# RWKV rounds of a hybrid decoder layer: activation functions grouped by table, the inversion's second half moved four slots, and two small reorderings

## The reference, cut to what matters

```
w_log = -softplus(-(w0 + tanh(xw) @ w2)) - 0.5 ; decay = exp(-exp(w_log))
a = sigmoid(a0 + xa @ a2) ; g = sigmoid(xg) @ g2
kk = k*k_k ; kk = kk * rsqrt(sum(kk*kk) + 1e-12) ; k = k*(1 + (a-1)*k_a)
# per token:  S = S diag(w) + (S a) b^T + v k^T ;  y = S r
y = (y - mean(y)) * rsqrt(var(y) + eps) * ln_w + ln_b + sum(r*k*r_k)*v
out = (y * g) @ w_out
```

## Time and profile before

| | us |
|---|---|
| median of 3 runs (lowest, highest) | 4605.08 (4598.61, 4607.50) |
| profiled execution, its own time | 4614.81 |
| its span | 4613.1 |
| PE busy | 4125.8 (89%) |
| DVE busy | 2521.4 (55%) |
| ACT busy | 1557.5 (34%) |
| mean granted TensorE clock | 0.95 |

### The profile page before, as it was taken

One profiled execution on the slowest core, in us unless ns is written; L12 is line 12 of the kernel. 1 busy time (PEld: TensorE's weight loads), 2 busy tenths in 40 slices (PEclk: granted clock), 3 DMA queues, 4 the chain that ended last, 5 costly groups with the idle time before them and its releaser, 6 DMA issues. The chain is left out here.

```text
span 4613.1 us, 84517 instructions
## 1 busy us (share of the span) xinstructions
PE 4125.8 (89%) x35797; PEld 3766.7 (82%) x35797; DVE 2521.4 (55%) x4994; ACT 1557.5 (34%) x2536; POOL 222.5 (5%) x161
## 2 busy tenths in 40 slices
PE   8789999989899999778768888886998899999998
PEld 4779989889888888778757777776976889999997
DVE  3344646332278884377846777764553255444446
ACT  3112222231176663221114555543541253111113
POOL 0000000000011110121200000000001100000000
PEclk9899999989899999889979999997999899999999
DMA  4322222233355553545530000004222221111112
GB/s 171 86 87 85 83 85 88 68 96 113 102 150 152 159 143 120 147 126 179 166 124 23 31 24 28 31 10 155 98 98 85 79 84 64 46 47 46 42 33 76
DMA packets 374262, 418.69 MB, mean 91 GB/s; under 512 B 49162, under 2 KB 315964, under 8 KB 373020
## 3 DMA queue, kind: packets, MB, share of 16 engines
q1 hardware_dynamic: 361599, 368.01, 26.1%
q0 software_dynamic: 7680, 27.97, 2.0%
q10 hardware_dynamic: 4608, 17.30, 0.9%
HBM read 289.10 MB, written 121.77 MB: 89 GB/s over the span
## 5 line engine op out<-in xcount | busy, mean ns | idle before, releaser
L1717 PE MATMUL bank<-sum_x_hi,sum_w_hi 128*128 128x352 f32 x768 | 262.3, 342 | 100.3 <-DVE sum_x_lo L1700 39.8
L210 PE MATMUL bank<-xn_hi,pz_whi 128*128 128x352 f32 (+1 forms) x984 | 328.4, 334 | 20.6 <-DVE pz_wlo L195 14.5
L210 PE MATMUL bank<-xn_hi,pz_wlo 128*128 128x352 f32 (+1 forms) x984 | 319.9, 325 | 0.0
L210 PE MATMUL bank<-xn_lo,pz_whi 128*128 128x352 f32 (+1 forms) x984 | 318.3, 323 | 0.0
L224 ACT ACTIVATE ring<-bank 128x352 f32<-128x352 f32 (+1 forms) x273 | 125.6, 461 | 541.4 <-PE bank L210 541.1
L3065 PE MATMUL bank<-bx_hi,bp_whi 128*128 128x384 f32 (+1 forms) x768 | 275.3, 358 | 32.7 <-DVE bx_lo L3123 19.7
L210 PE MATMUL bank<-xn_hi,pb_whi 128*128 128x352 f32 x816 | 275.1, 337 | 20.1 <-DVE pb_wlo L195 14.2
L210 PE MATMUL bank<-xn_lo,pb_whi 128*128 128x352 f32 x816 | 266.0, 326 | 0.0
L210 PE MATMUL bank<-xn_hi,pb_wlo 128*128 128x352 f32 x816 | 265.3, 325 | 0.0
L3686 PE MATMUL bank<-bx_hi,bp_whi 128*128 128x384 f32 (+1 forms) x768 | 251.7, 328 | 4.7 <-issue 4.7
L1717 PE MATMUL bank<-sum_x_hi,sum_w_lo 128*128 128x352 f32 x768 | 255.8, 333 | 0.0
(11 more groups left out here) (710 smaller groups left out, 12440.7 us busy)
## 6 DMA issues: line engine op xcount, KB each, us to landing
ring<-in_w_in_dram SPq DMA_DIRECT2D x90, 512.0 KB, 4.8
proj_scratch<-ring SPq DMA_DIRECT2D x66, 528.0 KB, 3.0
m_seg<-acum_scratch SPq DMA_DIRECT2D x32, 512.0 KB, 6.8
ring<-in_mlp_w_dram SPq DMA_DIRECT2D x16, 1024.0 KB, 5.5
ring<-in_mlp_w_dram SPq DMA_DIRECT2D x32, 512.0 KB, 3.4
gates_scratch<-ring SPq DMA_DIRECT2D x24, 528.0 KB, 4.6
merged_scratch<-sum_gate ACTq DMA_DIRECT2D x24, 528.0 KB, 5.1
m_raw<-proj_scratch SPq DMA_DIRECT2D x24, 512.0 KB, 5.7
```

The lines of the kernel that those rows point to most:

```text
L210: last = self.nc.tensor.matmul(ps[0:n, 0:m], w[:, q, 0:n], self.pair[x][:, q, t0:t0 + m], start=q == 0 and j == 0, stop=q == KD - 1 and j ...
L1717: last = self.nc.tensor.matmul(self.banks[e % n][:, 0:m], w[:, b % 2, q, :], self.pair[x][:, q, t0:t0 + m], start=q == 0 and i == 0, stop= ...
```

## The change

- **Activation functions.** Per period, Prepare's Ln stays near its place (slot 7), its Exp goes to slot 10, its three other exponentials to slots 11, 12 and 13; Finish starts much earlier in the period (mean in PE slot 4, centring in DVE slot 5, square in ACT slot 6, variance in PE slot 8), its Ln stands in ACT slot 9 and its Exp in slot 14. So the two logarithms are neighbours, and then the five exponentials.
- **Bank 7.** Its seven uses now come in the order decay, a, mean, key sum, variance, bonus, gate (PE slots 0, 2, 4, 6, 8, 14, 20), with waits to match. Prepare's DVE work that follows moves two or three slots later.
- **Inversion.** Half p=1 runs four slots later: its gram in slot 4, its last step in slot 26. The scan waits for p=0 before chunk 0 and for p=1 before chunk 4.
- **Gram masks.** On DVE the first mask product of a gram stays ahead of the scan's state and `r_R` copy of that slot, the other two (new function `vector_gram`) come behind them.
- **State.** The zeroing of the scan's state for a new pair of heads moves from the start of a period to slot 24 of the one before.

```diff
-STEPS = {p + (0 if s == 0 else 2 * s + 1): (s, p) for s in range(len(INVERSION)) for p in range(2)}
+STEPS = {(4 if s == 0 else 2 * s + 6) if p else (0 if s == 0 else 2 * s + 1): (s, p) for s in range(len(INVERSION)) for p in range(2)}
...
 # Prepare.tensor
         elif slot == 6:
             pe.wait_ge(self.a_ready, r + 1)
             pe.wait_ge(self.k_sq, r + 1)
+            if r >= 3:
+                pe.wait_ge(centred, r - 2)
...
-        elif slot == 12:
-            pe.wait_ge(self.k_rs, r + 1)
+        elif slot == 14:
+            pe.wait_ge(self.k_log, r + 1)
             pe.wait_ge(self.bon, r + 1)
+            if r >= 3:
+                pe.wait_ge(logged, r - 2)
...
 # Prepare.scalar
         elif slot == 7:
+            act.wait_ge(self.k_sum, r + 1)
+            activation(T[5], bank[:, :], ACT.Ln, bias=k.eps[:, 1:2]).then_inc(self.k_log, 1)
+        elif slot == 10:
+            act.wait_ge(self.k_log, r + 1)
+            activation(T[5], T[5], ACT.Exp, scale=-0.5).then_inc(self.k_rs, 1)
+        elif slot == 11:
             act.wait_ge(self.cum, r + 1)
-            activation(T[3], T[1], ACT.Exp, scale=-KAPPA)
-            activation(T[4], T[1], ACT.Exp, scale=KAPPA).then_inc(self.decays, 1)
-        elif slot == 8:
-            act.wait_ge(self.k_sum, r + 1)
-            activation(T[5], bank[:, :], ACT.Ln, bias=k.eps[:, 1:2])
-            act.drain()
-            activation(T[5], T[5], ACT.Exp, scale=-0.5).then_inc(self.k_rs, 1)
-        elif slot == 9:
+            activation(T[4], T[1], ACT.Exp, scale=KAPPA)
+        elif slot == 12:
+            activation(T[3], T[1], ACT.Exp, scale=-KAPPA).then_inc(self.decays, 1)
+        elif slot == 13:
             act.wait_ge(self.shifted, r + 1)
             activation(T[0], T[0], ACT.Exp, scale=-KAPPA).then_inc(self.exps, 1)
...
 # Invert: the last two mask products of a gram, emitted behind Scan.vector
+    def vector_gram(self, dve, r, slot):
...
+        tt(x.O[:, :, :], b0[:, :, 0:RC], mask(v.m_cross), ALU.mult)
+        tt(v.KX[:, r % 2, c, :], b1, mask(v.m_k), ALU.mult).then_inc(self.vs[p], 1)
...
 # Scan.vector
         elif slot == 24 and w:
...
             self.nc.vector.tensor_copy(v.SO[:, :], state[:, 0:RC]).then_inc(self.t_off, 1)
+            if r + 1 < ROUNDS:
+                self.nc.vector.memset(v.ST[:, 0, :], 0.0).then_inc(self.s_off, 1)
...
 # Finish.tensor
-        if slot == 15:
-            pe.wait_ge(bon_off, min(ROUNDS, r + 4))
+        if slot == 4:
+            pe.wait_ge(prepare.a_ready, min(ROUNDS, r + 4))
...
-        elif slot == 19:
+        elif slot == 8:
+            pe.wait_ge(prepare.k_log, min(ROUNDS, r + 4))
             pe.wait_ge(self.centred, r + 1)
...
-        elif slot == 23:
+        elif slot == 20:
+            pe.wait_ge(prepare.bon_off, min(ROUNDS, r + 4))
             pe.wait_ge(self.logged, r + 1)
```

More of the change, by code:

```diff
@@ L1111, in sync, with tensor @@
                 sp.dma_start(self.v.raw[:, i, :], self.k.proj[row:row + P, RW - 1:2 * RW]).then_inc(self.in_, 16)
-    def tensor(self, pe, r, slot, gated):
+    def tensor(self, pe, r, slot, gated, centred, logged):
         if not 0 <= r < ROUNDS:
@@ L1212, in vector @@
             stt(out=T[6], in0=pm[:, 0, :], scalar=col["rwkv_r_k"][:, j:j + 1], in1=T[7], op0=ALU.mult, op1=ALU.mult).then_inc(self.bon, 1)
-        elif slot == 11:
+        elif slot == 13:
             dve.wait_ge(self.k_rs, r + 1)
@@ L1216, in vector @@
             stt(out=T[1], in0=pm[:, 1, :], scalar=col["rwkv_k_k"][:, j:j + 1], in1=T[5], op0=ALU.mult, op1=ALU.mult)
-        elif slot == 12:
+        elif slot == 14:
             tt(T[2], T[2], T[4], ALU.mult)
-        elif slot == 13:
+        elif slot == 15:
             dve.wait_ge(self.bon_sum, r + 1)
             tt(v.bonus[:, r % 4, :], k.bank[7][:, :], pm[:, 2, :], ALU.mult).then_inc(self.bon_off, 1)
-        elif slot == 14:
+        elif slot == 17:
             dve.wait_ge(self.exps, r + 1)
@@ L1226, in vector @@
             tt(v.AR[:, x, :, RC:2 * RC], chunked(pm[:, 0, :]), chunked(T[3]), ALU.mult)
-        elif slot == 15:
+        elif slot == 18:
             self.nc.vector.tensor_copy(v.PC[:, x, :], chunked(T[3])[:, :, RC - 1])
             dve.drain()
-        elif slot == 16:
+        elif slot == 19:
             stt(out=v.AR[:, x, :, 0:RC], in0=chunked(T[1]), scalar=-1.0, in1=chunked(T[0]), op0=ALU.mult, op1=ALU.mult)
-        elif slot == 17:
+        elif slot == 20:
             tt(v.B[:, x, :, :], chunked(T[1]), chunked(T[2]), ALU.mult)
-        elif slot == 18:
+        elif slot == 21:
             tt(v.K[:, x, :, :], chunked(T[7]), chunked(T[4]), ALU.mult)
@@ L1315, in vector @@
             tt(v.ABR[:, w, c, :], wide(b0), mask(v.m_a), ALU.mult)
-            tt(x.O[:, :, :], wide(b0)[:, :, 0:RC], mask(v.m_cross), ALU.mult)
-            last = tt(v.KX[:, w, c, :], wide(b1), mask(v.m_k), ALU.mult)
+            return
         elif step == "square":
@@ L1332, in vector @@
         last.then_inc(self.vs[p], 1)
+    def vector_gram(self, dve, r, slot):
+        if not 0 <= r < ROUNDS or slot not in STEPS:
+            return
+        s, p = STEPS[slot]
+        if INVERSION[s][0] != "gram":
+            return
+        tt, v, x, c = self.nc.vector.tensor_tensor, self.v, self.v.inv[p], slice(p * BATCH, (p + 1) * BATCH)
+        b0, b1 = [bank[:, :].rearrange("p (i n) -> p i n", n=2 * RC) for bank in self.banks(p)]
+        mask = lambda m: m[:, :].unsqueeze(1).broadcast_to([P, BATCH, m.shape[1]])
+        tt(x.O[:, :, :], b0[:, :, 0:RC], mask(v.m_cross), ALU.mult)
+        tt(v.KX[:, r % 2, c, :], b1, mask(v.m_k), ALU.mult).then_inc(self.vs[p], 1)
     def scalar(self, act, r, slot):
@@ L1386, in tensor @@
             if sub == 0:
[L1387 to L1391, removed]
+                if c % BATCH == 0:
+                    p = c // BATCH
+                    pe.wait_ge(vs[p], (r + 1) * EACH["v"])
+                    pe.wait_ge(as_[p], (r + 1) * EACH["a"])
+                    if r and c == 0:
                         pe.wait_ge(self.y_off, r)
@@ L1416, in vector @@
         n, now = 8 * r + c, v.ST[:, c % 2, :]
-        if slot == 0 and not w:
+        if slot == 0 and r == 0:
             self.nc.vector.memset(now, 0.0).then_inc(self.s_off, 1)
@@ L1466, in __init__, with tensor @@
             S("summed"), S("centred"), S("squared"), S("varsum"), S("logged"), S("rstd"), S("gate"), S("gated"), [S("stored0"), S("stored1")])
-    def tensor(self, pe, r, slot, bon_off, y_off):
+    def tensor(self, pe, r, slot, prepare, y_off):
         if not 0 <= r < ROUNDS:
@@ L1492, in vector @@
         j, y = r // 2, v.y[:, r % 2, :]
-        if slot == 16:
+        if slot == 5:
             dve.wait_ge(self.summed, r + 1)
             stt(out=y, in0=bank[:, :], scalar=-1.0 / 64, in1=y, op0=ALU.mult, op1=ALU.add).then_inc(self.centred, 1)
-        elif slot == 22:
+        elif slot == 16:
             dve.wait_ge(self.rstd, r + 1)
@@ L1499, in vector @@
             tt(y, y, v.F[1], ALU.mult)
-        elif slot == 24:
+        elif slot == 22:
             dve.drain()
             ts(y, y, k.col["rwkv_ln_w"][:, j:j + 1], k.col["rwkv_ln_b"][:, j:j + 1], ALU.mult, ALU.add)
-        elif slot == 25:
+        elif slot == 23:
             dve.drain()
             tt(y, y, v.bonus[:, r % 4, :], ALU.add)
-        elif slot == 26:
+        elif slot == 24:
             dve.wait_ge(self.gate, r + 1)
@@ L1514, in scalar @@
         v = self.v
-        if slot == 17:
+        if slot == 6:
             act.wait_ge(self.centred, r + 1)
             self.nc.scalar.activation(v.F[0], v.y[:, r % 2, :], ACT.Square).then_inc(self.squared, 1)
-        elif slot == 20:
+        elif slot == 9:
             act.wait_ge(self.varsum, r + 1)
@@ L1557, in _ @@
                     scan.tensor(pe, q - 1, slot, invert.vs, invert.as_)
-                    prepare.tensor(pe, q + 1, slot, finish.gated)
-                    finish.tensor(pe, q - 2, slot, prepare.bon_off, scan.y_off)
+                    prepare.tensor(pe, q + 1, slot, finish.gated, finish.centred, finish.logged)
+                    finish.tensor(pe, q - 2, slot, prepare, scan.y_off)
         @block.vector
@@ L1566, in _ @@
                     scan.vector(dve, q - 1, slot)
+                    invert.vector_gram(dve, q, slot)
                     prepare.vector(dve, q + 1, slot, scan.read)
```

1 line of the change is left out of this document (added).

## The result

The changed kernel takes 4647.32 us (median of 3, 4647.15 to 4651.73) against 4605.08: a ratio of 1.0091, 95% interval 1.0073 to 1.0109. It is 42 us slower. The forecast was 4608 with a range up to 4631: the side and the size are both missed.

A forecast was written before the change was run, and what follows sets the result against it. PE's list sets the pace, 42.8 us a period. Stalls: 5.3 go, 6.6 come; clock gains 1.0: net +0.3 a period, +4 us over 14, first periods -1, so 4605 + 3 = 4608 us, range 4582 to 4631.

The forecast's parts named there:

- Own work of PE, and the list of waits: PE's own work in a period sums to 33.0 us; 9.8 us are stalls or a slow clock.
- What goes: Stalls removed per period: zeroing, table loads before inversion copies, last `r_U`, state updates and small things, 5.3 us in sum.
- Zeroing: PE's wait for the zeroed scan state, every second period, goes: 1.2 us a period gained.
- Decay product: At the first `r_U`, the sigmoid's table load is no longer covered by the p=1 gram: stall grows 1.75 us.
- key sum: PE's key sum waits for Finish's centring on DVE: some 1.65 us of stall, part at chunk 2's state.
- variance: Finish's variance on PE waits for Prepare's Ln on ACT: a stall of 1.5 us.
- Crossings: The last two p=1 crossings on DVE stand alone: PE waits 0.25 before the second, 1.45 before the third, 1.7 us.
- Split worth nothing: Splitting the gram masks on DVE brings `r_R` about 1.0 us earlier, but the later sigmoid holds `r_U`: costed at nothing.
- The clock: PE's clock falls after long idle times, 1.6 us each: 0.35 a period against 1.35 before, 1.0 us gained.
- Rival B: Slower: the clock falls behind the decay product in every period, 17 us more, 4625; chance 0.30 together with C.
- Rival A: Faster: one of the three new PE waits is absent because its queue is shorter, 4586 us; chance 0.28.
- Rival C: ACT's table loads were hidden anyway, so nothing is gained and losses stand; chance 0.30 together with B.

The follow-up runs named there:

- better version: The changed kernel with the inversion's second half (p=1) back at its old slots, activations grouped, masks split and zeroing early as changed: 4541.17 us, ratio 0.9862 to before.

## Why the prediction was wrong

- *Own work of PE, and the list of waits:* right. The walk has 43.1 - 0.35 = 42.75 us a period without the clock, and the estimate from the profile is 42.7. The sum of the stalls (+1.3 a period) came out as +1.2 by PE's idle time, or 42.7 - 41.1 = +1.6 by the clock.
- *What goes:* right. Zeroing, copies, last `r_U`. Zeroing was undervalued alone (30, where 1.2 x 14 and three falls of 1.6 make 22): with it fewer of the 2.58 are followed by a fall, too.
- *Decay product, key sum, variance:* right, 2.13, 0.68 with 0.86, 1.30 as idle times. *Crossings:* right where the last one waits 1.44 (1.6 of the 1.7), too large by 0.7 in every second period, where it waits 0.79; no wait before the one ahead of it shows.
- *Split worth nothing:* borne out on the better version (mean period 39.05 with it, 39.06 without).
- *The clock:* wrong, and this is the step that failed; it is nearly the whole miss. The step said "I take half, 0.35 a period, against 1.35: 1.0 gained". By the mean clock it is 3.7 after against 1.7 before: 2.0 lost (2.5 by PE's busy time). 3.0 a period over 14 is 42 us, and the time is 39 above the forecast. Three things were off in it, besides the count (13 falls in the 14 periods before, not 12). The 2.13 was taken as safer than 2.24 since it was shorter, yet the clock fell behind it in 9 of 12 periods. The price of a fall, 1.6 from the earlier trace rows, was taken as fixed. It held for a stretch at half clock of 3.4 us (9.1 against 7.5), but seven of the nine lasted twice as long, and one of these cost 3.1. And only one place was looked at: the last crossing's 1.44 or 0.79 (7 falls) and the waits before the key sum (3) bring falls too.
- *Rival B* was the mechanism in the main: the clock fell in three of four periods behind the decay product. But it gave an idle time of some 2.1 us as what decides, and falls stood behind 1.44 and 0.79 as well. It had 4625, with the 1.6 for each fall, and slower had 0.30, for B and C together. *Rival A* did not come: each of the three waits was there. *Rival C* is refuted: the grouping alone gains 46. The range was too narrow above for the same reason: the clock's term was bounded by its one price.

What stays open: why the clock fell behind the 2.13 in some periods and not in others, and why it then stayed at half for 3.4 us in some and 6.8 in others, which no run here separates; and how the clock's half of the 151 of the moved half alone divides among its waits, since only one of them was filled.

## What to carry to other kernels

In a schedule written by hand, look first for what a moved piece was covering: the gram had been the cover for a table load and a sigmoid, and the move uncovered them in each period. Price an idle time of the matmul engine with the clock that may follow it, and not by its length alone: count how often the clock falls behind it, for how long it stays down, and what other idle times stand near it. And when several edits go together, run the one line that moves most work alone: here it hid a gain of 65 us.

## What the runs showed of the hardware

- In the changed kernel an idle time of 2.13 us between dense stretches was followed by half clock in 9 of 12 periods, one of 1.44 in 4 of 6, and one of 0.79 three times. In the versions at the old slots with the early zeroing, with no wait above 1.31 in a period, the mean clock is 0.99 to 1.00.
- The length of one idle time does not settle it. The waits of 2.57 to 2.58 were followed by half clock 9 times of 13 in the kernel before, and 5 times of 13 when only the 2.24 elsewhere in every second period had gone.
- One fall cost 1.6 us of PE's time where half clock lasted 3.4 us, and 3.1 where it lasted 6.8.
- The Trainium skill (TensorE: Matmul & The Clock Gate, HAM oscillation) tells of a kernel that loses its clock in each round of a loop, by waits for DMA of 3 to 5 us. The pattern agrees with these runs, the length does not: here waits of 0.79 to 2.58 us on ACT and DVE were enough.
- Products whose result nobody reads, put into such an idle time, won 30 and 36 us.
- A table load takes the wait that is written last ahead of its activation: with the two waits exchanged it had ended 5.8 us before its activation started, and the idle time fell from 2.13 to 0.80.
